# A hybrid decoder step on one NeuronCore: the first pair of up tiles takes its weights row by row, with another order around it

## What is computed

```python
h = x + jnp.concatenate([o_g, o_d], axis=-1) @ w_out
hn = _rmsnorm(h, ffn_norm_g)
u, new_ffn = _causal_dwconv(hn @ w_up, ffn_buf, ffn_conv_w, ffn_conv_b)
y = h + (jax.nn.silu(u[..., :D_FF]) * u[..., D_FF:]) @ w_down
```

## Time and profile before

| | |
|---|---|
| median of 3 runs | 1638.8 us (1637.06 to 1640.02) |
| the profiled execution | 1636.91 us, span 1635.3 us from first to last instruction, granted clock 0.968 |
| PE busy | 1516.6 us, 93% of the span |
| DVE, ACT, POOL busy | 1053.3, 634.4, 395.5 us |
| units 0 to 15 | from about 771 to 879 us of the span |
| first up pair | from about 879 to 926 us |
| the other 21 pairs, then the down projection | to the end |

### The profile page before, as it was taken

How to read it: one execution, slowest core, us unless ns; L and a number is a source line. 1 busy time by engine, 2 the same in 40 slices (tenths; PEclk the granted TensorE clock), 3 DMA queues, 4 the chain that set the end, 5 groups by cost and what they waited for, 6 DMA issues and landing times.

```text
span 1635.3 us, 30132 instructions
## 1 busy us (share of the span) xinstructions
PE 1516.6 (93%) x11911; PEld 1430.3 (87%) x11911; DVE 1053.3 (64%) x1575; ACT 634.4 (39%) x1102; POOL 395.5 (24%) x750
## 2 busy tenths in 40 slices
PE   7999999998788888788998799999999999999998
PEld 6999999897567777554997799999999999999998
DVE  7445389786566676466457888877777777534320
ACT  6433332332344343453233434444444335423222
POOL 4000166563532252251002222222222220000000
PEclk8999999999799999898998899999999999999999
DMA  6311111232122311375632122222222226845433
GB/s 219 104 39 51 36 47 26 86 99 98 25 51 69 76 34 29 103 295 175 195 118 73 52 79 79 79 72 71 74 79 79 81 77 207 273 150 201 133 110 108
DMA packets 177981, 165.63 MB, mean 101 GB/s; under 512 B 24245, under 2 KB 157163, under 8 KB 176184
## 3 DMA queue, kind: packets, MB, share of 16 engines
q1 hardware_dynamic: 173528, 154.30, 30.5%
q0 software_dynamic: 1664, 6.29, 1.0%
q10 hardware_dynamic: 2656, 3.21, 0.5%
HBM read 125.68 MB, written 37.96 MB: 100 GB/s over the span
## 4 chain that ended last, share of the span: by engine, by line
PE 35%; DVE 5%; issue 4%; DMA 4%; ACT 3%; SPq 1%; POOL 0%; ACTq 0%; DVEq 0%; POOLq 0%
PE f_pair L3494 16%; PE f_pair L3541 15%; DMA up_raw<-in_w_up 3%; PE f_pair L3448 3%; ACT up_w_hi L2987 1%; DVE f_pre L3265 1%; DVE f_acc L3313 1%; ACT f_acc L3038 1%; DMA w_raw<-in_w_out 1%; DVE up_w_lo L3228 1%; DVE feat L3192 0%; DVE up_u L3265 0%; DVE m_xP_lo L3206 0%; ACT w_hi L2934 0%; DVE up_sums L3221 0%
## 5 line engine op out<-in xcount | busy, mean ns | idle before, releaser
L3494 PE MATMUL f_pair<-m_xP_hi,up_w_hi 128*128 128x264 f32 x1232 | 255.9, 289 | 16.3 <-DVE m_xP_lo L3206 10.5
L3494 PE MATMUL f_pair<-m_xP_lo,up_w_hi 128*128 128x264 f32 x1232 | 252.8, 287 | 0.0
L3494 PE MATMUL f_pair<-m_xP_hi,up_w_lo 128*128 128x264 f32 x1232 | 252.7, 287 | 0.0
L195 PE MATMUL proj<-x_hi,win_hi 128*128 128x352 f32 x672 | 220.1, 327 | 0.0
L195 PE MATMUL proj<-x_hi,win_lo 128*128 128x352 f32 x672 | 217.3, 323 | 0.0
L195 PE MATMUL proj<-x_lo,win_hi 128*128 128x352 f32 x672 | 216.9, 323 | 0.0
L3494 PEld LDWEIGHTS f_pair<-m_xP_hi,up_w_hi 128*128 128x128 f32 x1232 | 193.1, 190 | 20.5 <-issue 12.8
L3494 PEld LDWEIGHTS f_pair<-m_xP_lo,up_w_hi 128*128 128x128 f32 x1232 | 193.5, 191 | 0.0
L3494 PEld LDWEIGHTS f_pair<-m_xP_hi,up_w_lo 128*128 128x128 f32 x1232 | 193.0, 191 | 0.0
L3541 PE MATMUL f_pair<-dn_g_hi,dn_w_hi 128*128 128x352 f32 x528 | 171.8, 325 | 0.2 <-DVE f_pre L3265 0.2
L3541 PE MATMUL f_pair<-dn_g_lo,dn_w_hi 128*128 128x352 f32 x528 | 169.7, 321 | 0.0
(11 more groups left out here) (462 smaller groups left out, 2958.5 us busy)
## 6 DMA issues: line engine op xcount, KB each, us to landing
dn_raw<-in_w_down SPq DMA_DIRECT2D x50, 512.0 KB, 4.4
up_raw<-in_w_up SPq DMA_DIRECT2D x44, 512.0 KB, 5.0
win_raw<-in_w_in SPq DMA_DIRECT2D x28, 512.0 KB, 3.9
g_scratch<-f_prod SPq DMA_DIRECT2D x22, 528.0 KB, 2.7
dn_g_in<-g_scratch SPq DMA_DIRECT2D x66, 176.0 KB, 3.8
p_key<-in_cache_k SPq DMA_DIRECT2D x32, 256.0 KB, 3.7
w_raw<-in_w_out SPq DMA_DIRECT2D x16, 512.0 KB, 4.8
x_scratch<-feat SPq DMA_DIRECT2D x1, 4224.0 KB, 12.1
```

The lines of the kernel that those rows point to most:

```text
L195: mm = nc.tensor.matmul(out, w[:, k, :], x[:, k, g * TG:(g + 1) * TG], start=(k == 0 and i == 0), stop=(k == KT - 1 and i == 2))
L3494: mm = nc.tensor.matmul(pair[OF[name]][:, b, 0:HQ], w_[a][:, j, :], x_[t][:, j, b * HQ:(b + 1) * HQ], start=(name in FIRST_IN and j + x == ...
```

## The change

Five edits, all in `output_and_mlp`:

1. `up_in`, the semaphore of the up weights, becomes one for each row. For the first pair row 0 waits on SP for `low(14)` alone and row 1 for `low(15)`; before, both waited for `low(15)`. The casts for P1 and P2 wait for row 0 only, those for P4 for row 1, those of the sums for the sums.
2. The third, fourth and fifth weight operand of the first pair (for P5, P6, P7) are split one after the other ahead of the roots, on ACT and on DVE; before, the fourth and fifth stood between the token operands of P5, P6 and P7.
3. On PE all of P1 comes ahead of `totals(1)`, and `spread_roots(1)` comes behind the second step of P2 instead of the first.
4. `token_sums(j)` runs one step later, behind the low part j+1 of P5.
5. Conv rows are loaded on SP in the turns u = 1, 4, 6, 8 (before 1, 3, 5, 7) and turned on PE behind the units 2, 4, 6, 7 (before 1, 2, 3, 4); the copies on DVE move with them.

```diff
+    up_in = [sem(f"up_in_{n}") for n in ("gate", "value")]
...
+    ROWS_AT, ROWS_TURN = (1, 4, 6, 8), (2, 4, 6, 7)
...
             def load_up(p):
-                if p == 0:
-                    sp.wait_ge(split_lo, done(NO - 1))
-                else:
+                if p:
                     sp.wait_ge(sums_made, 4 * p)
                     sp.wait_ge(up_lo, turn(p - 1, "P4") + 1)
                 for s in range(2):
-                    sp.dma_start(up_raw[:, s, :, :], w_u[:, :, p * P + s * FF:(p + 1) * P + s * FF]).then_inc(up_in, 16)
+                    if p == 0:
+                        sp.wait_ge(split_lo, done(NO - 2 + s))
+                    sp.dma_start(up_raw[:, s, :, :], w_u[:, :, p * P + s * FF:(p + 1) * P + s * FF]).then_inc(up_in[s], 16)
...
-                if u in (1, 3, 5, 7):
-                    load_rows(u // 2)
+                if u in ROWS_AT:
+                    load_rows(ROWS_AT.index(u))
...
             def up_high(s):
-                act.wait_ge(up_in, 32 * (p + 1))
                 if name in S_NTH:
                     act.wait_ge(sums_made, 4 * p + S_NTH[name])
+                else:
+                    act.wait_ge(up_in[name == "P4"], 16 * (p + 1))
...
-            up_high(2)
+            for s in range(2, 5):
+                up_high(s)
             roots(1)
...
             for j in range(HK):
                 x_high("P5", j)
-            up_high(3)
             for j in range(HK):
                 x_high("P6", j)
-            up_high(4)
...
             def first_sums(p):
-                dve.wait_ge(up_in, 32 * (p + 1))
+                for s in range(2):
+                    dve.wait_ge(up_in[s], 16 * (p + 1))
...
-                if 1 <= u < 5:
-                    keep_rows(u - 1)
+                if u in ROWS_TURN:
+                    keep_rows(ROWS_TURN.index(u))
...
-            up_low(2)
+            for s in range(2, 5):
+                up_low(s)
             inverse(1)
...
                 x_low("P5", j)
                 scale(1, HK + j)
-                token_sums(j)
+                if j:
+                    token_sums(j - 1)
+            token_sums(HK - 1)
...
-            up_low(3)
             for j in range(HK):
                 x_low("P6", j)
-            up_low(4)
...
-                if 1 <= u < 5:
-                    turn_rows(u - 1)
+                if u in ROWS_TURN:
+                    turn_rows(ROWS_TURN.index(u))
...
-            product(0, "P1", range(0, 3))
+            product(0, "P1")
             totals(1)
-            product(0, "P1", range(3, 4))
-            product(0, "P2", range(0, 1))
+            product(0, "P2", range(0, 2))
             spread_roots(1)
-            product(0, "P2", range(1, 4))
+            product(0, "P2", range(2, 4))
```

More of the change, by code:

```diff
@@ L2701, in output_and_mlp @@
     rows_in, rows_turned, rows_kept = sem("f_rows_in"), sem("f_rows_turned"), sem("f_rows_kept")
-    up_in, sums_made, up_hi, up_lo, multiplied = sem("up_in"), sem("up_sums_made"), sem("up_hi"), sem("up_lo"), sem("up_multiplied")
+    up_in = [sem(f"up_in_{n}") for n in ("gate", "value")]
+    sums_made, up_hi, up_lo, multiplied = sem("up_sums_made"), sem("up_hi"), sem("up_lo"), sem("up_multiplied")
     u1_kept, kept_11, kept = sem("up_u1_kept"), sem("up_kept_11"), sem("up_kept")
```

## The result

| | median of the runs | range | runs |
|---|---|---|---|
| before | 1638.8 us | 1630.57 to 1645.21 | 11 |
| after | 1628.96 us | 1623.91 to 1631.02 | 11 |

After over before is 0.9944, with a 95% interval of [0.9925, 0.9962]. The change is faster, by 9.8 us as a difference of the medians and 9.2 us by the ratio.

The account below looks back on a forecast made before the run. PE was taken as the bound from 923.40 us, with waits and slow clock from 787 to 923 us to mend. Savings of 2.5 + 0.8 + 1.7 = 5.0 us gave a median of 1633.8 us, range 1630.0 to 1636.6.

Parts of the forecast that it names:

- from 923.40 us on the change has nothing to win: From 923.40 us, PE is busy 374.42 of 376.60 us at full clock, so no gain was expected there.
- the loads of the second pair bring nothing more: Behind P7, the second pair's loads are set off by the same remainder, so nothing more is won or lost.
- the first pair ahead of the scaling: From P1 to the second half's scaling in the first pair: scaling begins 0.8 us sooner, or 2.9 at full clock.
- my choice between two clocks: Behind P1, PE's 2.1 us rest was taken to bring 1.2 GHz: 0.8 us won, against 2.9 at 2.4 GHz.
- Rival (a): The clock stays up behind totals(1) in the first pair: 7.6 us saved, 1631.2 us; chance 0.25.
- Conv rows: In the units, the wait for conv rows and unit 5's slow stretch go, less exposed transposes: 2.5 us saved.
- rival (b): The 1.4 us idle time ahead of unit 2 brings a slow stretch: 3.3 us saved, 1635.5 us; chance 0.12.
- rival (d): Loads of units 5, 7 and 9 come late and hold PE: 4.7 us net slower, 1643.5 us; chance 0.03.
- rival (c): In the first pair totals(1) still waits, gaining only 0 to 0.8 us there: about 1635.9 us; chance 0.15.
- Token operands: From the first scaling to P6 and P7 in the first pair: 1.7 us saved at the slow clock, 2.2 fast.
- The forecast of 0.1 us for edit 4: Running token sums one step later only moves DVE's stand beside POOL: 0.1 us by the lock rule, 1.0 without.

Follow-up runs that it names:

- e1: The changed kernel, but in pairs 1 to 21 the casts for P1, P2 and P4 wait for both rows of up weights again; 1637.88 us, ratio 0.9971.
- e2: The kernel before, with one semaphore for each row of up weights in pairs 1 to 21 alone; 1634.01 us, ratio 0.9958.
- e9: The changed kernel with the two row loads of up weights swapped in pairs 1 to 21, so row 0 comes second; 1633.43 us, ratio 0.9947.
- e3: The changed kernel with conv rows loaded and turned where they were before; 1629.81 us, ratio 0.9930.
- e4: The changed kernel with the token sums back in the same step as the low part of P5; 1626.62 us, ratio 0.9904.
- e10: The changed kernel with the fourth and fifth weight operands split between the token operands again; 1627.70 us, ratio 0.9918.
- a2: The changed kernel unaltered, measured and profiled a second time on another chip beside a before of its own; 1624.84 us, ratio 0.9898.
- e5: The changed kernel with PE's order around the roots as before: totals(1) behind step 2 of P1, the spreading behind P2's first step; 1623.08 us, ratio 0.9899.
- e8: The changed kernel with P1 copied ahead of the roots, all scalings first, token sums between P6's low parts, t4 on DVE; 1622.87 us, ratio 0.9888.
- e6: The changed kernel, but in the first pair both rows wait for low(15) and the casts for both rows again; 1631.25 us, ratio 0.9922.

## Why the prediction was wrong

**The step that failed** is the sentence that from 923.40 us on the change has nothing to win, and with it the one that the loads of the second pair bring nothing more. That put edit 1 at zero in 21 of the 22 pairs; it is worth 4.8 us there in the profiled pair of executions, and between 4.8 and 9.6 by e1, e2 and e9. I had written down that the casts wait for one row only, and costed it where I was looking. The row that I leaned on, 374.42 busy of 376.60, had two signs against me. It leaves 2.2 us idle, which I took for nothing although the forecast as a whole was 5.0. And busy time of PE is modelled, so as much again hid inside it. The page of before had a third, which I did not use; its group of the casts (idle time and releaser at the end):

```profile
L2987 ACT CAST up_w_hi<-up_raw 128x512 fp32r<-128x512 f32 x66 | 40.7, 619 | 145.5 <-DMA up_raw<-in_w_up 145.5
```

Idle time of ACT costs nothing by itself. But a wait that comes in every pair and holds an instruction on DVE, ahead of the one that frees PE, can close a loop of its own, and here it did: one load followed the other by 20.64 us or more, where PE needs 20.50 for a pair. The plainest sign was in the chain from which the earlier trace rows are: I read it up to 907 us, and from 1121 to 1297 us it runs through nine loads in a row. e1, e2 and e9 show that the late cast is the cause. That the runs of before spread more than those of after (14.6 and 7.1 us) would fit a loop that holds PE in more pairs or fewer; no run tests it.

**The term that was mis-sized** is the first pair ahead of the scaling: 0.8 us, where P1 to the first scaling fell from 10.48 to 7.48 us, so 3.0. The mechanism went as told: the residual of unit 15 came 0.2 us behind P1's first matmul (880.60 and 880.40), the sums started at P1 + 2.92 (forecast 2.95), P2 at + 4.83 (5.05) after 0.88 us of idle PE (1.0). What fell was my choice between two clocks. The rest of 1.9 us from 883.3 to 885.2, with matmuls of one column in it, was not followed by 1.2 GHz before 891.4, nor was the same rest in e1, e3, e4, e9, e10 and a2. The two rows between which I chose lay at 1.4 and 2.5 us, and the forecast rest at 2.1; I took the row that was nearer by 0.3 us. Rival (a) held in this part, with 2.9 us. Of the edits it was edit 1 that counted: with PE's old order (e5) P1→P5 was 11.11 us, half a microsecond less than in after, so edit 3 was not needed.

**What was right.** Conv rows: 2.5 us forecast, 2.4 measured, and 2.3 by e3; 1.18 us of idle PE ahead of unit 2 (forecast about 1.4) brought no slow stretch, so rival (b) fell; the loads of units 5, 7 and 9 held nothing, so rival (d) fell; rival (c) fell at the residual. Token operands: P6 came 17.49 us behind the first scaling (forecast 17.5), of it 1.7 us for edit 2 (e10) and nothing for edit 4 (e4, forecast 0.1). P7 came 24.3 us behind the scaling in after and 23.5 in a2 (forecast 23.5 to 24.0); the 0.8 us between the two executions of one kernel lie in P6→P7, which ran partly at 1.2 GHz. The forecast of 0.1 us for edit 4 went by the exclusive lock of which the Trainium skill tells ("SBUF — State Buffer", section "SBUF: two separate sides"); without it, edit 4 would have been worth 1.0. The trace agrees with the lock: e4 measured 0.0, and whichever t2 meets POOL takes 1.7 us.

So by steps: conv rows 2.4 (2.5), first pair ahead of the scaling 3.0 (0.8), token operands 1.4 to 2.2 by the two executions (1.7), later pairs 4.8 (0). The forecast without its failed step, with rival (a) in the place of its clock, would have been 7.6 + 4.8 = 12.4 us; the stages of after give 11.6, and the medians 9.8. The 2 us between are no more than what the start of unit 0 varies by from execution to execution. The 16.7 us of a2 are 5 more than the stages. If its before lost 9.6 us in the pairs, as e1 did, the stages would come to 16.4; no profile of before on that chip shows it.

## What to carry to other kernels

An edit in a function that a loop calls is costed once for the loop's first pass and once for all the others, even if only the first was meant. Where PE is 99% busy, look for a wait that comes back in every pass and holds an instruction of another engine's queue, and follow the chain that ended last through the whole loop, not only through the stage that is being mended. Here the loop took at the least 0.14 us longer than PE's work on a pair, and a semaphore for each transfer instead of one for both was worth more (4.8 us and up) than any other part of the change. And when two edits are aimed at one stall, undo each alone: here edit 1 had removed the late sum, and edit 3, made for the same idle time, then cost 0.5 us.

## What the runs showed that was not expected

- Of two loads of 512 KB issued 0.4 us apart, the first landed 3.9 us after its issue and the second 5.2 us after its own (medians of the 21 later pairs of after), so a wait for both ends some 1.7 us later. In the slowest pair of before it took 7.5 us (1289.39 to 1296.90).
- DVE instructions with two operands in SBUF stood while POOL ran (1.68 against 0.71 us). The eight scalings of e8, which take one operand from PSUM, took 0.69 us each (5.49 in all), though POOL made its differences from 886.60 to 891.69. Two scalings of before with POOL idle took 1.43 us (at 859.74), so they did not stand.
- A rest of PE of 1.9 us between matmuls of full width at the end of P1 left the clock at 2.4 GHz for the next 6 us in seven profiles (after, a2, e1, e3, e4, e9, e10); in before, e2 and e6 rests of 2.5 to 2.8 us there were followed by 1.2 GHz.
